# Rotating queries and keys inside the projection loop, with the convolution taps cut into sequence halves

## The reference

```python
h = rmsnorm(x, mix_norm_w)
proj = h @ w_in                      # q, k, v, g, a, b, each 512 wide
# retention, 4 heads of 128: y = masked, decayed (q k^T) v, forward and backward
q = rotary(q, positions)             # [x1 cos - x2 sin, x2 cos + x1 sin]
k = rotary(k, positions) * 128 ** -0.5
y_ret = silu(g) * group_norm(retention_f(q, k, v) + retention_b(q, k, v))
# convolution group
u = a * sigmoid(b)
y_conv = silu(layernorm(depthwise_conv31(u) + conv_b))   # 31 taps along the tokens
x = x + concat(y_ret, y_conv) @ w_out
x = x + cross_attention(rmsnorm(x), rmsnorm(mem))        # 4 heads, 256 memory tokens
x = x + relu(rmsnorm(x) @ w_ff1) ** 2 @ w_ff2
return rmsnorm(x, final_norm_w)
```

## Time and profile before

| | before |
|---|---|
| median of 3 runs | 2965.84 us (2965.05 to 2968.18) |
| profiled execution, its own time | 2963.24 us |
| span of that execution | 2961.3 us |
| mean granted TensorE clock | 0.979 |
| PE, DVE, POOL, ACT busy | 95%, 47%, 30%, 18% of the span |
| one iteration of the projection loop | 156.1 us |
| from 695 us to 945 us (end of projection, retention, first mix) | 250 us |

### The profile page before, as it was taken

The page is one execution under the profiler, slowest core; times in us unless marked ns, Lnnn a source line. Parts: engine busy times, 40 slices in busy tenths (PEclk is TensorE's granted clock), DMA queues, the critical chain, the costliest instruction groups (busy, mean ns, idle before and its releaser), DMA issues.

```text
span 2961.3 us, 37392 instructions
## 1 busy us (share of the span) xinstructions
PE 2820.0 (95%) x14026; PEld 2384.1 (81%) x14026; DVE 1393.5 (47%) x1550; ACT 537.9 (18%) x934; POOL 889.7 (30%) x443
## 2 busy tenths in 40 slices
PE   5899999996898999999999999989999999999997
PEld 4788888885887898888888888779988888888885
DVE  4593939396675433532414234553336233151444
ACT  5211111112354322100101001232221000010012
POOL 1243424244762100333323333220003333332330
PEclk8999999998899999999999999999999999999998
DMA  4133333336654223111111113132221111111111
GB/s 158 50 118 118 113 113 111 117 117 237 208 163 135 79 86 100 43 50 45 48 50 50 43 49 106 57 121 93 86 78 47 45 50 50 43 49 50 50 42 64
DMA packets 289750, 253.93 MB, mean 86 GB/s; under 512 B 8016, under 2 KB 253960, under 8 KB 283400
## 3 DMA queue, kind: packets, MB, share of 16 engines
q1 hardware_dynamic: 266320, 203.45, 22.5%
q10 hardware_dynamic: 23352, 49.39, 4.5%
HBM read 196.71 MB, written 56.10 MB: 85 GB/s over the span
## 4 chain that ended last, share of the span: by engine, by line
PE 76%; DVE 15%; DMA 3%; issue 3%; ACT 2%; POOL 1%; DVEq 0%; ACTq 0%; SPq 0%; POOLq 0%
PE ps L678 21%; PE ps L673 21%; PE ps L674 21%; DVE acc L1588 10%; PE ps L1033 2%; PE ps L1035 2%; PE ps L1034 2%; PE ps L897 1%; DMA wqk_d<-pst 1%; DMA out<-rows 1%; DVE alo L1875 1%; PE ps L1044 0%; DMA wb<-wqk_d 0%; DVE zfin L1901 0%; PE ps L995 0%
## 5 line engine op out<-in xcount | busy, mean ns | idle before, releaser
L537 POOL TENSOR_SCALAR whi<-wraw 128x1024 fp32r<-128x1024 f32 x192 | 231.8, 1207 | 1899.8 <-PE ps L678 1183.2
L673 PE MATMUL ps<-ahi,whi 128*128 128x512 f32 x1376 | 541.2, 393 | 13.4 <-DVE alo L1875 11.6
L674 PE MATMUL ps<-alo,whi 128*128 128x512 f32 x1376 | 536.8, 390 | 0.0
L539 POOL TENSOR_TENSOR wlo<-wraw,whi 128x1024 fp32r<-128x1024 f32 x192 | 530.3, 2762 | 16.0
L673 PE MATMUL ps<-bhi,whi 128*128 128x512 f32 x1024 | 399.4, 390 | 2.3 <-DVE blo L1796 2.3
L674 PE MATMUL ps<-blo,whi 128*128 128x512 f32 x1024 | 398.4, 389 | 0.0
L1588 DVE SCALAR_TENSOR_TENSOR acc<-upad,taps,acc 128x2048 f32<-128x2048 f32 x120 | 346.6, 2888 | 15.7 <-DVE acc L1585 0.6
L678 PE MATMUL ps<-ahi,wlo 128*128 128x512 f32 x1376 | 340.2, 389 | 0.0
L1887 DVE TENSOR_TENSOR res<-ps,res 128x512 f32 x128 | 88.6, 692 | 519.7 <-PE ps L678 519.7
L673 PE MATMUL ps<-xhi,whi 128*128 128x512 f32 x768 | 305.1, 397 | 18.7 <-DVE xlo L1519 11.2
L673 PEld LDWEIGHTS ps<-ahi,whi 128*128 128x128 f32 x1376 | 259.2, 188 | 72.3 <-DVE alo L1875 14.9
(11 more groups left out here) (259 smaller groups left out, 3624.0 us busy)
## 6 DMA issues: line engine op xcount, KB each, us to landing
wraw<-in_w_ff SPq DMA_DIRECT2D x128, 512.0 KB, 3.9
proj_d<-st ACTq DMA_DIRECT2D x64, 256.0 KB, 2.5
wraw<-in_w_in SPq DMA_DIRECT2D x24, 512.0 KB, 4.4
xt<-in_x SPq DMA_DIRECT2D x16, 512.0 KB, 6.1
wraw<-in_w_xkv SPq DMA_DIRECT2D x16, 512.0 KB, 5.5
vwo_d<-pst ACTq DMA_DIRECT2D x16, 512.0 KB, 3.7
wqk_d<-pst ACTq DMA_DIRECT2D x16, 512.0 KB, 4.1
wraw<-in_w_out SPq DMA_DIRECT2D x16, 512.0 KB, 5.2
```

Source lines behind the costliest of these rows:

```text
L537: pool.tensor_scalar(whi[:, slot, :, :], wraw[:, slot, :, :], 1.0, 0.0, ALU.mult, ALU.add).then_inc(w_hi, 1)
L539: pool.tensor_tensor(wlo[:, slot, :, :], wraw[:, slot, :, :], whi[:, slot, :, :], ALU.subtract).then_inc(w_ready, 1)
L673: nc.tensor.matmul(o, whi[:, slot, k, :], hi(k), start=(k == order[0]), stop=False)
L674: nc.tensor.matmul(o, whi[:, slot, k, :], lo(k), start=False, stop=False)
```

## The change

- **Rotation moves into the projection loop.** ACT takes a chunk of q or k into `st`, sends it with the two halves of the partitions exchanged to the new buffer `swp` (two transfers), loads the chunk of both tables into `rope`, and stores the rotated chunk. DVE multiplies `st` by the cosine (`cosine`), POOL `swp` by the sine (`swapped`), DVE adds (`rotate`). Eight chunks for each `c`.
- **Taps on halves.** Each of the 31 taps is run first on tokens 0 to 1007, and after all of these on tokens 1008 to 2047: 62 instructions. Seven of them (for `c` over 0) stand before `gated(3)`. SP waits for the 62nd where it waited for the 31st.
- **Tables once.** They are computed for all 2048 tokens in the iteration `c` = 0.
- **Retention stage.** No table and no swapped copy is loaded, the four products on POOL and the two sums on DVE for each head are gone; `load_k(0)` and `load_v(0)` are issued behind the last tap, before the end of the projection. Keys, values and queries of a head have one buffer each. Values and keys go through three banks instead of two.
- **Convolution norm.** POOL adds the four channel tiles (`conv_sums`) and the four tiles of squares (`square_sums`); PE does one product for the means where it did four, and four small ones for the variances where it did sixteen.
- Constants (`cen_mat`, `io_c`, `zeta`) are made earlier, the order of ACT and DVE in the heads is changed accordingly, and buffers are placed anew.

```diff
             def proj_splits(c):
...
                 proj_split(c, "O0", done(c, "a3"))
+                swapped(c, 0)
                 proj_split(c, "k", 1 + 2 * c + 1, o_mm)
+                swapped(c, 1)
+                swapped(c, 2)
                 proj_split(c, "O1", done(c, "q3"))
+                swapped(c, 3)
+                swapped(c, 4)
                 proj_split(c, "v", 1 + 2 * c + 2, o_mm)
+                swapped(c, 5)
+                swapped(c, 6)
                 proj_split(c, "K0", done(c, "k3"))
+                swapped(c, 7)
...
+                def rotated(i):
+                    wait_alone(act, st_rot, 8 * c + i + 1)
+                    n = i % 4
+                    act.dma_start(proj_d[4 * (i // 4) + c, :, n * NC:(n + 1) * NC], st[:, n, :]).then_inc(st_st[n], 16)
+                    if i + 2 < 8:
+                        rope_load(i + 2)
+                def rotary(*items):
+                    for i in items:
+                        name, n, u = "qk"[i // 4], i % 4, i % 2
...
+                        src, left = evacuated(name, n)
+                        act.activation(st[:, n, :], src, ACT.Copy).then_inc(left, 1)
+                        if i >= 2:
+                            wait_alone(act, st_rot, 8 * c + i - 1)
+                        bank_left(act, c, f"{name}{n}")
+                        half = P // 2
+                        act.dma_start(swp[0:half, u, :], st[half:P, n, :]).then_inc(swp_in[u], 16)
+                        act.dma_start(swp[half:P, u, :], st[0:half, n, :]).then_inc(swp_in[u], 16)
+                        if i:
+                            rotated(i - 1)
...
-                store("q", 0, 0, 1, 2, 3)
-                store("k", 4, 0, 1)
+                rotary(0, 1, 2, 3, 4, 5)
                 wait_alone(act, o_mm, 1 + 2 * c + 2)
                 made(0)
-                store("k", 4, 2)
+                rotary(6)
                 made(2)
-                store("k", 4, 3)
-                store("v", 8, 0, 1)
+                rotary(7)
+                store("v", 8, 0)
+                rotated(7)
+                store("v", 8, 1)
...
+                for i, last in enumerate((13, 19, 22, 25, 28, 31, 34, 37)):
+                    taps_to(last)
+                    cosine(i)
+                    taps_to(last + 1)
+                    rotate(i)
+                    if i == 4:
+                        made_low(0)
+                        made_low(1)
+                    if i == 6:
+                        made_low(2)
+                        made_low(3)
+                taps_to(40)
+                low("K0", 2, khl[:, 0])
+                query_low(0)
+                taps_to(54)
+                low("K1", 3, khl[:, 1])
+                query_low(1)
+                taps_to(STEPS)
...
             def conv_means(h):
-                pe.wait_ge(c_in[h % 2], 16 * (h // 2) + 16)
-                for c in range(CT):
-                    last = pe.matmul(ps[:, 3, :], mean_mat[:, :], cvs[h % 2][:, c, :], start=(c == 0), stop=(c == CT - 1))
-                last.then_inc(c_me, 1)
+                pe.wait_ge(c_sm, 3 * h + 3)
+                pe.matmul(ps[:, 3, :], mean_mat[:, :], c_sum[:, :], start=True, stop=True).then_inc(c_me, 1)
```

More of the change, by code:

```diff
@@ L133, in build @@
             acc = alloc(s1, "acc", [P, S], F32)
-            alloc(s1, "k_room", [P, 2528], F32)
+            with ExitStack() as over:
+                pos_i = alloc(over, "pos_i", [P, S], I32)
+            with ExitStack() as over:
+                ang = alloc(over, "ang", [P, S], F32)
+            rope = alloc(s1, "rope", [P, 2, 2, NC], F32)
+            alloc(s1, "k_room", [P, 480], F32)
             vhl = alloc(s1, "vhl", [P, 2, 2, M], F32R)
@@ L137, in build @@
                 khl = alloc(over, "khl", [P, 2, 2, M], F32R)
+            swp = alloc(s1, "swp", [P, 2, NC], F32)
             with ExitStack() as over:
-                pos_i = alloc(over, "pos_i", [P, NC], I32)
-            ang = alloc(s1, "ang", [P, NC], F32)
-            turns = alloc(s1, "turns", [P, NC], F32)
+                turns = alloc(over, "turns", [P, S], F32)
             pst = alloc(s1, "pst", [P, 2, 2, NC], F32R)
@@ L1272, in _ @@
                 made(6)
+            project(0)
+            with act.Fori(1, HEADS) as c:
+                project(c)
+            act.wait_ge(iot_c, 2)
+            for h in range(HEADS):
+                for d in range(2):
+                    act.activation(zeta[:, d, h:h + 1], io_c[:, d:d + 1], ACT.Exp, scale=lg[:, 5, d, h:h + 1]).then_inc(dec_act, 1)
+            act.activation(gch[:, :, :], lg[:, 5], ACT.Exp, scale=float(P)).then_inc(dec_act, 1)
             leave_phase(act)
-            act.wait_ge(iot, 6)
+            act.wait_ge(iot, 2)
             for h in range(HEADS):
                 for d, xi in ((0, xi_f), (1, xi_b)):
-                    s = lg[:, 5, d, h:h + 1]
-                    act.activation(xi[:, h, :], io_s[:, d, :], ACT.Exp, scale=s).then_inc(dec_act, 1)
-                    act.activation(zeta[:, d, h:h + 1], io_c[:, d:d + 1], ACT.Exp, scale=s).then_inc(dec_act, 1)
-            act.activation(gch[:, :, :], lg[:, 5], ACT.Exp, scale=float(P)).then_inc(dec_act, 1)
+                    act.activation(xi[:, h, :], io_s[:, d, :], ACT.Exp, scale=lg[:, 5, d, h:h + 1]).then_inc(dec_act, 1)
             def key_evac(h):
@@ L1554, in _, with project @@
             dve.wait_ge(pad_ok, 2)
-            with dve.Fori(0, HEADS) as c:
+            def project(c):
                 def gated(n):
@@ L1592, in turn, with taps_of @@
                 def turn(m, ins):
                     ins.then_inc(tab, 1)
-                    dve.wait_ge(tab, 9 * c + m + 1)
-                dve.wait_ge(conv_step, 1 + TAPS * c)
-                low("V0", 0, vhl[:, 0])
-                dve.wait_ge(tab_in, 16 * c + 32)
+                    dve.wait_ge(tab, m + 1)
+                def taps_of(first, last):
+                    for m in range(first, last):
+                        tap(m)
+                dve.wait_ge(conv_step, 1 + STEPS * c)
@@ new lines, in project @@
+                low("V0", 0, vhl[:, 0])
+                if isinstance(c, int):
+                    tables(turn)
+                gated(0)
+                gated(1)
+                if not isinstance(c, int):
+                    bank_left(dve, c, "a1")
+                    taps_of(0, 1)
+                low("V1", 1, vhl[:, 1])
+                if not isinstance(c, int):
+                    taps_of(1, 4)
+                gated(2)
+                if not isinstance(c, int):
+                    taps_of(4, 7)
@@ new lines, in project, with taps_to @@
+                gated(3)
+                bank_left(dve, c, "a3")
+                at = 0 if isinstance(c, int) else 7
+                def taps_to(last):
+                    nonlocal at
+                    taps_of(at, last)
+                    at = last
+                for i, last in enumerate((13, 19, 22, 25, 28, 31, 34, 37)):
[9 more added lines that the diff above has]
+                        made_low(3)
@@ L1598, in _, with tables @@
+                taps_to(40)
[5 more added lines that the diff above has]
+                taps_to(STEPS)
+                for m in range(4, 8):
+                    made_low(m)
+            def tables(turn):
+                dve.wait_ge(tab_in, 32)
                 turn(0, dve.tensor_copy(ang[:, :], pos_i[:, :]))
@@ L1608, in _ @@
                                                  op0=ALU.mult, op1=ALU.max))
-                gated(0)
-                gated(1)
-                low("V1", 1, vhl[:, 1])
-                gated(2)
-                gated(3)
-                bank_left(dve, c, "a3")
-                def taps_of(first, last):
-                    for t in range(first, last):
-                        tap(t)
-                taps_of(0, 16)
-                made_low(0)
-                made_low(1)
-                taps_of(16, 18)
-                made_low(2)
-                made_low(3)
-                taps_of(18, 21)
-                low("K0", 2, khl[:, 0])
-                query_low(0)
-                taps_of(21, TAPS)
-                low("K1", 3, khl[:, 1])
-                query_low(1)
-                for m in range(4, 8):
-                    made_low(m)
+            project(0)
+            with dve.Fori(1, HEADS) as c:
+                project(c)
             dve.sem_inc(bank_free, G_HALF0 + G0)
```

365 lines of the change are left out of this document (175 added, 190 removed).

## The result

The changed kernel takes 3083.3 us (median of 4 runs, 3079.3 to 3087.3) against 2965.7 (2965.05 to 2968.18): a ratio of 1.0397, 95% interval 1.0381 to 1.0412. The prediction had 3026 and at most 3070. It is slower, as forecast, but by 118 us and not by 60. The mechanism that was forecast is there; where the other half comes from is the question of this study. "The changed kernel" is always this one; times of the experiments are medians, beside runs of the kernel before on the same chip (2964 to 2966 us).

What follows compares the result with a forecast made beforehand. DVE's tap chain, then the next b load, was taken to bound projection iterations, with 1.2 us slack. Projection +104 and retention -44 on 2963.2 gave 3023, as a median 3026 us; eight in ten within 2972 to 3070.

Steps and rivals of the forecast that it cites:

- The clock at `b0`: Projection, iteration starts: idle before b0 leaves PE at half clock, 3 us for each of three iterations, 9 us.
- the loss to the splits: DVE's tap chain: taps beside POOL's operations run longer, 16.2 us over 30 taps, unchanged by the change.
- Waits of DVE for `swp` to land and for ACT to pass its own waits: DVE chain in the projection: shown by no row, from nothing to 5 us, taken as 2.
- hidden in the larger one: Projection, v2: ACT's late bank costs 15.5 us in the last iteration; elsewhere the larger stall covers it.
- I take half, 14 us: Retention heads: fewer products for means and variances save up to 7 to 8 us a head, 30 in all; half counted.
- the 12 us for the values: Retention start: first values some 9 us behind g3 instead of 20.6; gain 12 us, from 6 to 16.
- head 0's wait for keys: Retention start: of the 5.5 us wait part stays, since key_tokens waits for the last made_low; gain 4.
- Rivals 1 and 2: Whole kernel: 1, only unavoidable costs, 2972 us, chance 0.13; 2, half taps let POOL in sooner, 2941 us, chance 0.08.
- Rival 3: Retention stage gives only 20 us: values come no sooner and scans set the heads; 3050 us, chance 0.12.
- Rival 4: Projection: clock falls longer, 8 us an iteration, +15; 3041 us, chance 0.10.
- Rival 5: Projection: POOL's operations cost DVE their whole length, a sine product 1.25 us for 1.0; 3062 us, chance 0.12.
- Rival 2: Projection: with half taps a split waits at most 1.2 us and DVE loses half; 2941 us, chance 0.08.

Runs made afterwards that it cites:

- e1: Changed kernel with SP loading the next iteration's b weights and first values before it waits for the last tap: 3045.6 us.
- e2: Changed kernel with ACT writing the exchanged halves into swp straight from PSUM instead of two transfers: 3055.8 us.
- e3: Changed kernel with all of the rotation left out (part of the computation omitted), halved taps kept: 2980.5 us.
- g1_half: f2_order with v_in where no tap reads, loaded behind K1; zeta, gch and xi moved; in the last head ACT squares the convolution's last tile earlier: 2969.2 us.
- e4: Changed kernel with the next head's values, keys and queries issued before SP waits for the normalised convolution chunk's store: 3066.8 us.
- r1_norm_on_pe: Changed kernel with the convolution norm's sums back on PE, no additions on POOL: 3069.6 us.
- h1_sp_order: g2_full with SP's store of conv_d behind the next iteration's a and V1 loads: 2946.2 us.
- h2_sp_half: h1_sp_order with taps in halves again, seven of them ahead of gated(3): 2953.2 us.
- e5: Changed kernel with the 31 taps whole and none ahead of gated(3), rotation and loads kept: 3073.7 us.
- f2_order: Changed kernel with the edits of e1, e2 and e4, plus cosines, low halves and last made_low moved among DVE's taps: 2975.2 us.
- g2_full: g1_half with the 31 taps whole and none ahead of gated(3), cosines and low halves placed accordingly: 2963.5 us.

## Why the prediction came out as it did

**Right: what sets an iteration.** The chain on DVE, behind it the `b` load, behind it `b0`: e1 took away the waits before `b0` (26.8 us and the clock behind them), and e2 made the chain 7.2 us shorter. The clock at `b0` was forecast at 3 us an iteration; from `b0` to `gated(3)` iteration 2 takes 53.6 us instead of 50.2, 3.4 more. The half taps, the low halves and the loss to the splits cost in sum what the rows had said (96.3 for 97.0, from e3). A cosine or a sum takes 0.68 us, as the rows had said, where nothing disturbs it; nine of the sixteen in iteration 2 took 1.5 to 2.9, beside POOL.

Of the 56 us by which the profiled execution is over the forecast, 24 lie in the projection, 28 in the retention stage and 4 behind it (noise, as far as can be told). A step failed in each of the two stages.

**Wrong in the projection: "Waits of DVE for `swp` to land and for ACT to pass its own waits [...]: from nothing to 5, I take 2".** They were 12.6 us (6.2 for `swp`, 3.6 for K1, 2.4 for `pst`, 0.4 others). The chain sums as 96.3 + 13.1 + 12.6 and a rest of 5.0 for the eight sine products, where 8 had stood: 127.0 for 120.1. The transfer that fills `swp` was never priced, though it sits between ACT and two other engines on the chain; and DVE's order was taken as given, when every fixed position in it is a wait as soon as one of the two engines runs at another pace. The 3.6 us for K1 are such a wait: PE is late from K0 to v2 on and partly below the full clock, so K1 is late, and DVE stands still for it. With it failed the sentence that in iterations other than the last the stall at v2 "is hidden in the larger one". The stall before K0 (4.2 to 7.6 us), behind a sine product that waits for `swp`, stood nowhere in the prediction. The sum has one slip besides: the 95.5 us count from the first tap and not from `gated(3)`, 0.3 us, and 358.4 less 343.1 for the last iteration are 15.3 and not 15.5.

**Off in size: the projection, +128.0 for +104.** The excess by iteration is 4.1 in iteration 0 (37.1 for 33), 6.2 and 9.0 in the next two (32.6 and 35.4 for 23.4 and 3 of clock), 4.4 in the last (22.9 for 15.5 and 3). In iteration 2 it is 6.6 of chain (127.0 for 120.1, less the slip of 0.3), 2.0 between last tap and `b0` (10.9 for 8.9) and 0.4 of clock. In the last iteration PE waits 6.3 us before K0, which the forecast of 15.5 us for v2 alone didn't hold.

**Wrong in the retention stage (-15.6 for -44): "Up to 7 to 8 a head, 30 in all [...] I take half, 14 us", and the 12 us for the values.**

- Up to the first states: 27.4 us behind `g3` instead of 33.8, so 6.4 where "values" and "head 0's wait for keys" had 16. The values came 8.8 us sooner, but the states wait for ACT, which goes through `made(6)`, `zeta` and `xi` before it takes a value out. g1_half moved those, and the states came at 10.2 us.
- From the first states of head 0 to those of head 1: 36.6 for 53.5, 16.9 gained where 14 and a share of the norm's 14 had stood. Right.
- From there to head 2, to head 3 and to the mix: 43.6, 43.3 and 41.9 for 42.2, 40.5 and 38.5, a loss of 7.6 where a gain of 10 was forecast. e4 turns it into a gain of 3.9 (38.1, 38.7, 40.5). What failed is "I take half, 14 us": I had read from PE's side how short the products get, and not what new order SP and ACT have around them. The size was off too. The 6.82 us for sixteen small products come from the stretch at a clock of 0.50; in r1_norm_on_pe they take 3.9 us a head, in the changed kernel four take 1.2, and PE saves 5.3 us a head where 7 to 8 had stood.

**The rivals.** Rivals 1 and 2 gave 2972 and 2941 us, far below. Rival 3 came true for its stage (15.6 us instead of 20), though not because values came no sooner. Rival 4's 8 us of clock at each `b0` did not come (3.4 in iteration 2), but the clock also fell at K0 to v2. Rival 5 did not come true as a price for each operation: by it a sine product costs DVE 1.25 us, and the rest above leaves 5.0 us for eight, some 0.6 each. This is a rest between two kernels and not a row. The rows show both cases: where a cosine and a product wait for the same `swp` and start together, DVE loses 1.1 us (1.80 for 0.68 at 588.70, beside a product of 1.26 at 588.69). The rule of the Trainium skill (SBUF — State Buffer, section SBUF: two separate sides) agrees with such a row, and with the second mask above, which has two inputs in SBUF. Taken at a whole instruction each time, it says more than these chains show. Rival 2's idea, that half taps are good for something, isn't borne out: whole taps are faster by 7.0 us (h1_sp_order against h2_sp_half) and 9.6 (e5).

**Behind all of it** stands one sentence of the prediction that was true of this order and false of the work: that whatever is added to DVE lengthens the iteration. In h1_sp_order DVE does the same rotation, at 114 us busy in 156, and the iteration is not longer at all. In the projection the change was slow because a load, four low halves and the rotations stood behind taps that nobody was waiting for, and because the exchanged halves came by transfer.

What stays open: how the 5.0 us of the sine products and the 15.5 us of the splits divide, since both are rests of sums, and which of f2_order's moved places gave how much of its 37 us. Nothing was tried against the last 24.6 us between the taps' end and the first scan.

## What to carry to other kernels

An engine at 70% that "sets" the period may only be holding the wrong things behind its long chain. Before pricing added work at its length, list what stands behind the chain in every queue (here SP's next load, ACT's next bank, POOL's split of K0, the low halves) and ask which of it could go ahead. And price each hop between engines that a moved step adds, transfers first: DVE's operations were forecast within 4%, its waits for the hops at a sixth.

## What the runs showed of the hardware

- Two transfers that exchange the 64-partition halves of a 512-column chunk in SBUF took 2.2 to 6.3 us to landing in one iteration (median 4.5), and DVE waited up to 5.8 us for them. ACT can write the exchanged half of a bank straight from PSUM into the other partitions; this took 27.5 us off the kernel (22.8 by the profiled executions).
- In g2_full the mean granted clock over 7 us was 0.59 behind an idle stretch of 4.55 us, 0.77 behind one of 4.52 and 0.76 behind one of 3.88. Taking the three away gave 17.3 us, more than their 13.0 us of idleness.
- GpSimd's products of 512 columns between taps cost VectorE some 0.6 us each (a rest, not a row), half of the 1.25 us that one takes alone; one that started together with a VectorE product cost it 1.1 us.
- Two VectorE operations on 128 columns took 4.40 and 4.48 us beside GpSimd products on 2048 columns of 4.63 and 4.49 us (h1_sp_order, 724 to 733 us), where the same operations took 0.29 and 0.35 us just before.
